# A long convolution in rounds of 256 channels: ScalarE's scaled copies one group ahead, VectorE's taps, product and differences in that order, TensorE's magnitude sums between the two ways back

## The reference

```python
    filt = (hdn @ w4.astype(F32)).reshape(T, 2, D_INNER)
    filt = filt * jnp.exp(-t * deltas[None, :])[:, None, :]
    filt = filt / (jnp.sum(jnp.abs(filt), axis=(0, 1), keepdims=True) + HY_FILTER_EPS)
    return filt[:, 0], filt[:, 1]
...
    taps = jnp.concatenate(
        [h_fwd, jnp.zeros((1, h_fwd.shape[1]), F32), h_bwd[:0:-1]], axis=0)
    y = jnp.fft.irfft(jnp.fft.rfft(vf, n=n, axis=1) * jnp.fft.rfft(taps, n=n, axis=0)[None],
                      n=n, axis=1)[:, :T]
    return (y + vf * skip.astype(F32)).astype(v.dtype)
```

## Time and profile before

| what | value |
| --- | --- |
| median of 3 runs | 2404.24 us (2402.88 to 2405.18) |
| the profiled execution's own time | 2406.78 us |
| its span | 2405.0 us |
| mean granted TensorE clock | 0.964 of full speed |
| rounds c = 1 to 6 of the convolution | 458.90 to 687.40 us of the span |

### The profile page before, as it was taken

The page is one execution under the profiler, slowest core; times in us unless marked ns, Lnnn a source line. Parts: engine busy times, 40 slices in busy tenths (PEclk is TensorE's granted clock), DMA queues, the critical chain, the costliest instruction groups (busy, mean ns, idle before and its releaser), DMA issues.

```text
span 2405.0 us, 36878 instructions
## 1 busy us (share of the span) xinstructions
PE 2236.0 (93%) x15305; PEld 1855.4 (77%) x15305; DVE 1367.0 (57%) x2335; ACT 1004.5 (42%) x1832; POOL 618.4 (26%) x520
## 2 busy tenths in 40 slices
PE   7999999898999989999999989889989999699998
PEld 7999999888999989899999867856776677333332
DVE  4455546788872566666666667789455664411112
ACT  4344334444432455655656553435433432211112
POOL 1111123555541132322323201203220111133331
PEclk9999999899999999999999989999988999799999
DMA  5322332110014223222222224312331143799993
GB/s 182 103 74 88 101 116 79 44 36 19 32 54 135 62 69 82 71 74 78 72 69 80 54 53 102 103 36 75 86 113 49 32 126 116 268 367 376 371 377 145
DMA packets 226337, 274.78 MB, mean 114 GB/s; under 512 B 41192, under 2 KB 193737, under 8 KB 213626
## 3 DMA queue, kind: packets, MB, share of 16 engines
q1 hardware_dynamic: 210330, 256.68, 33.4%
q0 software_dynamic: 15264, 13.65, 1.8%
q10 hardware_dynamic: 576, 2.10, 0.2%
HBM read 305.18 MB, written 23.13 MB: 137 GB/s over the span
## 4 chain that ended last, share of the span: by engine, by line
PE 67%; DVE 17%; ACT 8%; issue 4%; DMA 2%; POOL 1%; SPq 0%; DVEq 0%; POOLq 0%; ACTq 0%
PE ps L93 15%; PE ps L94 14%; PE ps L95 14%; PE ps L4073 7%; PE ps L4116 4%; PE ps L1884 2%; ACT sp L115 2%; ACT whi L99 1%; DVE wlo L103 1%; DVE prods L1198 1%; PE ps L3189 1%; DVE fsum L1021 1%; PE ps L4043 1%; PE ps L3056 1%; DVE p L2182 1%
## 5 line engine op out<-in xcount | busy, mean ns | idle before, releaser
L93 PE MATMUL ps<-hn_h,whi 128*128 128x264 f32 (+2 forms) x2256 | 690.9, 306 | 26.7 <-DVE wlo L103 7.7
L95 PE MATMUL ps<-hn_h,wlo 128*128 128x264 f32 (+2 forms) x2256 | 672.9, 298 | 0.0
L94 PE MATMUL ps<-hn_l,whi 128*128 128x264 f32 (+2 forms) x2256 | 672.5, 298 | 0.0
L93 PEld LDWEIGHTS ps<-hn_h,whi 128*128 128x128 f32 x2256 | 431.4, 191 | 51.9 <-issue 18.2
L94 PEld LDWEIGHTS ps<-hn_l,whi 128*128 128x128 f32 x2256 | 431.6, 191 | 9.5 <-issue 0.2
L95 PEld LDWEIGHTS ps<-hn_h,wlo 128*128 128x128 f32 x2256 | 430.0, 191 | 11.5
L103 POOL TENSOR_TENSOR wlo<-wraw,whi 128x2048 fp32r<-128x2048 f32 (+1 forms) x44 | 158.3, 3598 | 464.0 <-ACT whi L99 464.0
L99 ACT ACTIVATE whi<-wraw 128x2048 fp32r<-128x2048 f32 (+1 forms) x134 | 202.4, 1511 | 43.9 <-PE ps L95 37.4
L103 DVE TENSOR_TENSOR wlo<-wraw,whi 128x2048 fp32r<-128x2048 f32 (+1 forms) x90 | 172.7, 1919 | 50.3 <-ACT whi L99 50.1
L4073 PE MATMUL ps<-ex_raw,xT 128*64 128x512 f32 x600 | 135.5, 596 | 0.0
L766 DVE SCALAR_TENSOR_TENSOR c<-ub,vec,c 128x528 f32<-128x528 f32 x48 | 45.6, 949 | 122.5 <-ACT c L115 122.5
(11 more groups left out here) (704 smaller groups left out, 5312.0 us busy)
## 6 DMA issues: line engine op xcount, KB each, us to landing
ex_raw<-in_w_gate_up SPq DMA_DIRECT2D x49, 1024.0 KB, 8.0
wraw<-in_hy_w_in SPq DMA_DIRECT2D x32, 1024.0 KB, 5.6
wraw<-in_da_w_in SPq DMA_DIRECT2D x64, 512.0 KB, 4.3
ex_raw<-in_w_down SPq DMA_DIRECT2D x26, 1024.0 KB, 7.5
wraw<-in_w_gate_up SPq DMA_DIRECT2D x15, 1024.0 KB, 7.5
wraw<-in_w_in SPq DMA_DIRECT2D x14, 1024.0 KB, 5.5
wraw<-in_hy_w_out SPq DMA_DIRECT2D x8, 1024.0 KB, 7.6
wraw<-in_da_w_out SPq DMA_DIRECT2D x8, 1024.0 KB, 8.2
```

The lines of the kernel that those rows point to most:

```text
L93: e.matmul(out, lhsT=l[0], rhs=r[0], start=start, stop=False)
L94: e.matmul(out, lhsT=l[0], rhs=r[1], start=False, stop=False)
L95: return e.matmul(out, lhsT=l[1], rhs=r[0], start=False, stop=stop)
```

## The change

Three orders change; no instruction is added, removed or resized, and GpSimd's and SyncE's lists stay as they are.

- ScalarE makes `hc` of group z+1 before it rounds `Y_h` of group z. Before, `hc` of group z stood right ahead of VectorE's product of group z.
- VectorE does, per group: `hp` of the step, the product of the group, and only then the halves' sums and differences and the larger magnitudes. Step 4 moves behind them, and the third block's differences and the weights' sums (`vector_w4`) move behind `vector_turned` and the third block's larger magnitudes.
- TensorE does the sums of magnitudes between `tensor_back` of half 0 and of half 1.
- Ahead of round 0, the weights of round 1 are prepared earlier on VectorE and ScalarE.

```diff
             tensor_back(e, w, c, 0)
+            if c < 7:
+                tensor_filter_end(e, w, c + 1)
             tensor_back(e, w, c, 1)
             tensor_back_end(e, w, c, 0)
             tensor_back_end(e, w, c, 1)
-            if c < 7:
-                tensor_filter_end(e, w, c + 1)
...
     def scalar_conv(e, w):
         scalar_unit(e, w, (7, 3, 1), hy_step[7, 3, 1])
+        scalar_w4(e, w, 1)
         scalar_sums(e, w, 0)
-        scalar_w4(e, w, 1)
         for c in range(8):
+            scalar_freq(e, w, c, 0)
             for z in range(5):
-                if c + z == 0:
-                    scalar_freq(e, w, 0, 0)
                 if c < 7:
                     scalar_filter(e, w, c + 1, z if z < 4 else 5)
-                if c + z:
-                    scalar_freq(e, w, c, z)
-                if c < 7 and z == 4:
+                if z < 4:
+                    scalar_freq(e, w, c, z + 1)
+                elif c < 7:
                     scalar_turned(e, w, c + 1)
-                elif c == 7 and z == 2:
+                if c == 7 and z == 2:
...
             vector_differ(e, w, 0, 2)
+            vector_w4(e, w, 1)
             vector_larger(e, w, 0, 2)
...
-        vector_w4(e, w, 1)
         for c in range(8):
             n = c + 1
             for z in range(5):
-                if c + z == 0:
-                    vector_freq(e, w, 0, 0)
                 if c < 7:
                     vector_filter(e, w, n, z if z < 4 else 5)
-                    if z in (1, 3):
-                        vector_differ(e, w, n, z // 2)
+                vector_freq(e, w, c, z)
+                if c < 7 and z in (1, 3):
+                    vector_differ(e, w, n, z // 2)
+                    vector_larger(e, w, n, z // 2)
                     if z == 3:
                         vector_filter(e, w, n, 4)
-                    elif z == 4:
-                        vector_differ(e, w, n, 2)
-                if c + z:
-                    vector_freq(e, w, c, z)
-                if c < 7 and z in (1, 3):
-                    vector_larger(e, w, n, z // 2)
...
+            if c < 7:
+                vector_turned(e, w, n)
+                vector_larger(e, w, n, 2)
+                vector_differ(e, w, n, 2)
             if c < 6:
                 vector_w4(e, w, c + 2)
             if c < 7:
-                vector_turned(e, w, n)
-                vector_larger(e, w, n, 2)
                 vector_sums(e, w, n, 0)
```

## The result

The changed kernel takes 2471.2 us (2470.3 to 2476.3, 4 runs) against 2403.6 us (2402.4 to 2405.2) before: ratio 1.0285, interval 1.0267 to 1.0303. It is 68 us slower. The forecast was slower, with 2433 us and a range up to 2448: the sign is right, the size is not.

The account below looks back on a forecast made before the run. Bound by TensorE and VectorE, two nearly full engines handing work to each other. +4.5 us a round times 6 is +27; with rounds 0 and 7, +29 on 2406.8 gives 2436, median 2.5 lower: 2433 us, range 2412 to 2448.

Parts of the forecast that it names:

- The tail's order: Tail, from way back to next round's first signal product: 9.6 to 14.2 us by order alone, +4.6 a round.
- The clock in the tail: TensorE at half clock after the tail's wait and one-column sums: +1.5 us a round, bounds 1.2 to 1.7.
- GpSimd's holding: VectorE held on the shared port, `Y_l` 0 over `rr` of group 1: +0.3 us a round (0 to 1.9).
- the middle's clock: Half clock on up to 3.8 us of matmuls after TensorE's wait for step 4: +0.8 us a round (0 to 1.5).
- t: Time in us counted from the round's first signal product; step 4 was forecast to end at 22.0.
- the walk: Round 3's durations stepped through the new orders; it ended the middle at 25.8 us.
- The middle: From a round's first signal product to the way back: 28.6 to 25.8 us by order, a gain of 2.8.
- The sum: Per round: 1.9 by order, 1.5 and 0.8 for clock, 0.3 for GpSimd: +4.5 us, times 6 is +27.
- Round 0: Early weights remove a 3.88 us wait, way back 3 to 4 us earlier, tail costs 4.6 plus 1.5: +1.5 taken.
- Round 7: Last round, without filter work: `Y_h` 3 comes later behind `hc` 4, way back 0 waits: +0.5 us.
- slower by more: Rival: port's full 1.9 and the clock's upper ends, 7.0 us a round, +38 to +50 in all; chance 0.13.
- The rival "faster": Middle gains more than tail loses, needing step 4 by t = 20.2 and no half speed; about 2392 us, chance 0.08.

Follow-up runs that it names:

- e16: Changed kernel with 24 unused matmuls of 256 columns added on TensorE between way back 0 and the sums of magnitudes: 2455.9 us.
- e9: Changed kernel with GpSimd's two `yl` pieces of the last round moved from groups 0 and 1 to behind the groups: 2451.3 us.
- e3: Kernel before with VectorE's loop of the change alone, without the early weights: 2447.8 us, ratio 1.0175.
- e6: Changed kernel with `hc` of group 4 behind the magnitudes of step 4, and the sums of magnitudes back at the round's end: 2442.2 us.
- e14: e6 with GpSimd's two `yl` pieces moved behind the groups: 2440.4 us.
- e17: e6 with VectorE's step 4 and the differences of block 1 back ahead of product 3: 2406.4 us, ratio 1.0006.
- e5: Changed kernel with ScalarE's `hc` of group 4 moved behind the magnitudes of step 4: 2456.4 us.
- e1: Kernel before with TensorE's part alone, the sums of magnitudes between the ways back of the halves: 2456.9 us, ratio 1.0214.

## Why the prediction was right in sign and wrong in size

- **The tail's order, +4.6: right.** The chain `hc` 4, `Y_h` 3, magnitudes, step 5, product 4, low parts, larger magnitudes, sums, way back 1, read-out is in the timeline as walked. Where the clock stayed full (e16, round 2) the tail took 14.31 us; the forecast without clock was 14.2. VectorE's step 5 waited 7.4 us and not 5.8, since step 5's taps and the 28 matmuls ahead of the copy took 5.3 us (587.07 to 592.38, granted clock 0.68) and not 3.8.
- **The clock in the tail, 1.5 forecast: this step failed.** I took it from stretches of 3.0 and 3.4 us in the rows of before and bounded it at 1.7. But the changed tail was at half clock from the sums to the end of way back 1, 10.7 us in round 3 (597.67 to 608.33). Against e16's 14.31 it cost 3.8 a round. TensorE's waits there were even shorter than forecast (1.47 and 0.19 us ahead of and in the sums, where I had 3). Rows after one wait or one set of sums can't bound what follows when both come together: here TensorE is idle for two of the tail's first seven us and then has the sums.
- **GpSimd's holding, 0.3 forecast (0 to 1.9), and the middle's clock, 0.8: this step failed too.** Against these 1.1 together e9 shows 3.3 us a round for the `yl` pieces alone: 1.8 is VectorE's busy time (23.56 to 21.73), the rest goes with TensorE's waits for the steps 2 and 4 (2.22 and 2.92 us, in e9 none and 2.00) and the half clock behind the latter (granted 0.94, in e9 1.00). I had looked at one collision (`Y_l` 0 over `rr` of group 1) and priced clock and port apart, though the one brings the other. Step 4 ended at 587.0, t = 24.6, not 22.0: `rr` of group 0 is held by GpSimd's `gg` as well, both `rr` of group 1 in turn by `Y_l` and `yl`, and the larger magnitudes by `Y_l` 1. With `yl` gone and the clock full the middle was 26.2; the walk gave 25.8. That is in part luck: the walk has 0.9 us for a held correction, which then ran free (0.40 us), and in e9 other pieces of GpSimd's still hold `rr`.
- **The middle, forecast to gain 2.8 by the order: near the mark only without `yl` and half clock (e9).** VectorE's order alone made it 5.4 longer (e3), and with the copies of groups 1 to 3 ahead it is still 4.8 longer (e6), so they hide little of that. In the changed kernel it is 1.1 longer; most of what lies between is the granted clock, 0.85 in e6's usual middle and 0.94 here (by the estimate above 5.0 us lost against 1.8).
- **The sum.** 4.5 a round were forecast, 9.7 found. The tail is 2.5 longer than forecast (18.2 against 15.7), nearly all by its clock; the middle 2.7 (29.6 against 26.9), by GpSimd and what follows from it. Round 0: the weights' wait at 422.25 turned into one of 3.75 us for step 0, so its way back came only 0.9 us earlier and not 3 to 4, and its tail cost 8.6 instead of 6.1. Round 7 gained 1.5 where 0.5 was to be lost.
- **The range** ended at 2448, and even the rival "slower by more", with the upper ends of clock and port (7.0 us a round), ended at +50. It named the right two causes; their upper ends were too low.
- **The rival "faster"** needed step 4 at t = 20.2; it came at 24.6. That the fullest engine's input should start sooner held for `prods`: its waits fell to a third. The time went up because other inputs of that engine became later.

What stays open: how much of e6's 33.2 is step 4's place by itself, how much the half clock that comes with its wait, and how much GpSimd's holding. e14 and e17 give 2.4 and 4.9 us less, but by different edits, and neither holds the clock fixed. Open too is what the narrow matmuls of the sums have to do with the half clock of the tail. Nor was it tried to give the larger magnitudes another buffer.

## What to carry to other kernels

On an engine that works in order, a copy taken one group ahead also waits for its producer one group ahead. Everything behind it inherits that wait, so look at what stands between the moved instruction and its old place, not at the instruction. Here that copy was the smaller part (15 us, e5): the sums, moved into the middle of a stretch where TensorE had no wait, cost 52 us by themselves (e1), as they brought a wait, an uncovered read-out and half clock at once. So a move into a full stretch needs the clock and everything the old place covered in its sum. And a step that frees the only bank its producer has (step 4) has to come as early as it can: moving it behind a product and the larger magnitudes cost 36 us (e17).

## What the runs showed of the hardware

- Work added to TensorE made the kernel faster: with 24 matmuls a round in an idle stretch the kernel took 15 us less. In one tail of seven the granted clock stayed at 1.00 through way back 1 (3.04 us against 5.22), in the others less of it was at half clock (as 4.57 us at 0.63).
- Two middles of one execution (e6) with the same order and about the same waits took 30.68 us at a granted clock of 0.94 and 33.58 at 0.85.
- VectorE's operations with two SBUF inputs and GpSimd's take turns: 0.42 us became 1.54 (573.45) when GpSimd's `yl` started between two `rr`. Moving two GpSimd pieces of 1.3 us a round took 3.3 us off the middle, the half clock that went with them included.
